# adaLN by column-tiled fp32 products spread over the layers, norms as diagonal products with a scale and a shift per feature

## The chip, the cores and the metric

One NeuronCore of a Trainium2 chip runs the whole program in one launch. The metric is device time in microseconds. Five engines work side by side, each through its own instructions in order: TensorE (PE, matrix products), VectorE (DVE), ScalarE (ACT), GpSimd (POOL, here mostly an issuer of DMAs) and SyncE (SP, which issues the loads of the weights). They hold each other up through semaphores: a count that one engine raises and another waits for.

## The reference, cut to what matters

Two transformer layers over 128 context tokens and 256 latent tokens, in fp32. Each layer derives six vectors of 1024 values, for the context and for the latent tokens, from a conditioning vector, and uses them around its two sublayers:

```python
def _adaln(cvec, w, b):
    m = (jax.nn.silu(cvec) @ w + b).reshape(-1, 1, 6 * D_MODEL)   # w: 1024 x 6144
    return jnp.split(m, 6, axis=-1)

mp, ms = _adaln(c_ctx, mod_w[i], mod_b[i]), _adaln(c, mod_w[i], mod_b[i])
hs = _rmsnorm(xs, norm1_g[i]) * (1 + ms[1]) + ms[0]      # the same for hp with mp
xs = xs + ms[2] * mixer(hs)
hs = _rmsnorm(xs, norm2_g[i]) * (1 + ms[4]) + ms[3]
xs = xs + ms[5] * ffn(hs)
```

Layer 0's mixer is windowed attention beside retention (one input projection of 2816 columns), its second half a dense SwiGLU. Layer 1's mixer is neighbourhood attention, its second half a top-2-of-8 expert SwiGLU, chosen by a router (`h @ w_router`, 1024 x 8, then top 2). One RMSNorm ends it.

## The kernel before, in words

The 384 tokens are three tiles of 128 rows (tile 0 context, 1 and 2 latent). A dense product runs on blocks of 128 x 1024 fp32 weights (512 KB). SP loads them into a ring of six raw buffers (`rawb`), ScalarE rounds each to `whi` (fp32r) and VectorE takes the rest, `wlo = raw - whi` (lines 464 and 469, three buffers each), and TensorE makes three products for one: hi x hi, lo x hi, hi x lo (lines 519 to 521). The experts do the same at lines 488 and 492 with eleven raw buffers, and besides run their overflow tokens by plain fp32 products on the raw block, 32 stationary columns wide, four side by side in the array (lines 1224 and 1242). Engines take blocks strictly in a numbered order.

The stages, in order: the twelve 512-column chunks of layer 0's adaLN (48 blocks, a loop at lines 1290 to 1299); two chunks of layer 1's (8 blocks); norm 0; the input projection, in whose block order the other 40 adaLN blocks of layer 1 stand two behind each weight block (`mod1`, lines 885 and 887); retention; attention of layer 0; output projection; norm 1; dense SwiGLU; norm 2; the QKV projection; attention of layer 1; output projection; norm 3; router; experts; last norm.

An adaLN block is converted like any other. Its products have the conditioning columns as stationary operand (hi and lo of both vectors) and stream 512 columns, two k-slices for each of hi and lo: four products. The rows go from PSUM to `mst`, and by a POOL DMA to `mods_scratch` in DRAM; from there POOL loads them back as rows of `mrow` (lines 705, 711, 717).

A norm (`norm_rows`, line 1746; `norm` on TensorE, line 870) works on token rows. TensorE spreads the scale and shift rows over 128 partitions by products with selector matrices (line 834), VectorE forms `h = x * rstd * scale` and `h + shift` for each tile (lines 1758 and 1764, 128 x 1024 each), TensorE turns `h` (line 866), ScalarE and VectorE make `hT_hi` and `hT_lo` out of PSUM, TensorE spreads the gate rows, and then the next product starts. `rstd` comes from ScalarE's squares of all three tiles (line 1380), one VectorE scaling (line 1748), one ScalarE root (line 1382), one reciprocal. The router takes 72 products that have the turned tokens as stationary operand and stream 8 columns.

Of the kernel before, what the change touches and what calls it, by code (L numbers as in the profile page):

```python
# [7 lines left out]
F32 = mybir.dt.float32  # L8
# [49 lines left out]
MOD_CH, MOD_STEP = 12, 3  # L58
B_MOD0 = 0
B_MOD1 = B_MOD0 + MOD_CH * SB  # L60
MOD_EARLY, MOD_PER = 2, 2
IN_BLOCKS = IN_EVEN * KD // BLK
B_OUT0 = B_MOD1 + MOD_CH * SB + IN_BLOCKS

N_MOD1, N_IN = [B_MOD1 + b for b in range(MOD_EARLY * SB)], []
while len(N_MOD1) + len(N_IN) < MOD_CH * SB + IN_BLOCKS:
    N_IN.append(B_MOD1 + len(N_MOD1) + len(N_IN))
    for _ in range(min(MOD_PER, MOD_CH * SB - len(N_MOD1))):
        N_MOD1.append(B_MOD1 + len(N_MOD1) + len(N_IN))
assert len(N_IN) == IN_BLOCKS and SB % MOD_PER == 0  # L70
# [5 lines left out]
assert IN_EVEN % 512 == 256 and EB % RAW == 0 and EB % HL == 0 and (MOD_STEP * SB) % RAW == 0  # L76
# [4 lines left out]
TURNED = {0: 0, 1: 6, 2: 9, 3: 15, 5: 21}  # L81
# [5 lines left out]
for _name, _n in (("ident", P), ("ones", P), ("before", P), ("slots", CAP), ("experts", E), ("orow", E), ("sel", 4 * P),  # L87
# [7 lines left out]
def constants():  # L95
# [15 lines left out]
    sel = np.zeros((4, 32, 4, P))  # L111
    for m, rows in enumerate(((0, 2, 4), (1, 3, 4), (0, 2, 4, 5), (1, 3, 4, 5))):
        for r in rows:
            sel[:, r, m] = 1
    put("sel", sel.reshape(P, 4 * P))
# [26 lines left out]
def build(nc, a, outs):  # L142
# [5 lines left out]
    mods = nc.dram_tensor("mods_scratch", [4, 2 * MOD_CH * 512], F32).ap()  # L148
# [4 lines left out]
    with ExitStack() as ctx:  # L153
# [27 lines left out]
        mrow = sb("mrow", [P, D])  # L181
        gate = sb("gate", [P, 2, D])
        gbc = sb("gbc", [P, D])
# [31 lines left out]
        moe_top = top[0] + 4 * BLK  # L215

        top[0] = act_at + 12 * 1024
        wr = sb("wr", [P, KD, E])
        wr_hi = sb("wr_hi", [P, KD, E], F32R)
        wr_lo = sb("wr_lo", [P, KD, E], F32R)  # L220
# [14 lines left out]
        ccol = sb("ccol", [P, 16])  # L235
        padrow = sb("padrow", [C_HEADS * DR, PADW])
        mst_at = act_at + 10 * 1024
        mst = sb("mst", [4, MOD_STEP, 512], at=mst_at)

        top[0] = act_at  # L240
        mr_hi = sb("mr_hi", [P, D], F32R)
        mr_lo = sb("mr_lo", [P, D], F32R)
        sel_r = sb("sel_r", [P, 4 * P], F32R)
# [8 lines left out]
        mst1 = sb("mst1", [4, 512])  # L252
# [56 lines left out]
        ident = cst("ident")  # L309


        cs_by_k = cs4[:, 0:4 * KD].rearrange("p (k c) -> p k c", c=4)


        w_loaded = [sem(f"w_loaded{i}") for i in range(RAW)]
# [1942 lines left out]
```

## Time and profile before

| | |
|---|---|
| median of 3 runs (lowest, highest) | 2025.83 us (2024.74, 2027.09) |
| the profiled execution: its own time, its span | 2025.68 us, 2023.6 us |
| PE busy, share of the span | 1800.2 us, 89% |
| DVE busy | 1231.9 us, 61% |
| ACT busy | 1074.8 us, 53% |
| moved by DMA, mean rate | 440.91 MB, 218 GB/s |
| mean granted TensorE clock | 0.935 |

A busy time is the time in which an engine had an instruction under way. The granted clock is a share of full speed (1.0 is 2.4 GHz, 0.5 is 1.2 GHz). All times of the trace are counted from the start of the span; the 2.1 us between span and time lie around it.

### The profile page before, as it was taken

Reading aid. Unit: us, or ns where it says so; the run is one execution under the profiler, and the core shown is the slowest. Engines: PE = TensorE matmul, PEld = TensorE weight load, DVE = VectorE, ACT = ScalarE, POOL = GpSimd, SP = SyncE. Lnnn points to the kernel's source line nnn. Section 1 sums busy time; section 2 is a strip of 40 time slices with the busy share of each in tenths; the row PEclk is TensorE's granted clock in tenths of the full one; section 3 lists DMA queues with packets and bytes.
Section 4 is the critical chain, followed back from the end, with each engine's and each line's share of the span. In section 5 each row is a group of like instructions: output and inputs, shape, how many; then the busy total and the mean of one; then the engine's idle time right before and its main releaser. Section 6 shows DMA issues by size and latency. Waiting matters only on the chain.

```text
span 2023.6 us, 26720 instructions
## 1 busy us (share of the span) xinstructions
PE 1800.2 (89%) x9765; PEld 1375.9 (68%) x9766; DVE 1231.9 (61%) x1430; ACT 1074.8 (53%) x1451; POOL 162.5 (8%) x262
## 2 busy tenths in 40 slices
PE   4868888889999989999799999999898989899890
PEld 2546676668888868767676656667676767677670
DVE  3764556653434252484446556578787878788783
ACT  3755543533332233463245545567676777677771
POOL 3010010030000040160010000000000000000002
PEclk9879997989999979999589999999999999999995
DMA  8946650158443445321168777799999989899883
GB/s 271 324 176 227 220 195 13 40 170 301 125 121 119 125 115 138 106 71 57 69 219 234 234 228 239 230 312 334 330 336 323 338 310 364 308 348 326 315 296 108
DMA packets 204805, 440.91 MB, mean 218 GB/s; under 512 B 16648, under 2 KB 36160, under 8 KB 204672
## 3 DMA queue, kind: packets, MB, share of 16 engines
q1 hardware_dynamic: 188928, 394.31, 58.4%
q0 software_dynamic: 15744, 44.73, 6.9%
q8 instruction: 95, 1.56, 0.3%
q14 instruction: 38, 0.31, 0.1%
HBM read 413.69 MB, written 25.30 MB: 217 GB/s over the span
## 4 chain that ended last, share of the span: by engine, by line
PE 74%; DVE 11%; ACT 7%; issue 4%; DMA 3%; POOL 0%; SPq 0%; ACTq 0%; DVEq 0%; POOLq 0%
PE ps L519 22%; PE ps L520 20%; PE ps L521 20%; PE ps L1224 3%; DMA rawb<-in_mod_w 2%; DVE wlo L469 2%; DVE wlo L492 2%; ACT whi L464 2%; ACT whi L488 2%; PE ps L968 1%; PE ps L1242 1%; PE ps L1187 1%; DVE h L1758 1%; PE ps L834 1%; DVE h L1764 1%
## 5 line engine op out<-in xcount | busy, mean ns | idle before, releaser
L469 DVE TENSOR_TENSOR wlo<-rawb,whi 128x1024 fp32r<-128x1024 f32 x224 | 269.6, 1223 | 346.6 <-ACT whi L464 345.5
L492 DVE TENSOR_TENSOR wlo<-rawb,whi 128x1024 fp32r<-128x1024 f32 x288 | 348.1, 1223 | 163.5 <-ACT whi L488 161.7
L464 ACT ACTIVATE whi<-rawb 128x1024 fp32r<-128x1024 f32 x224 | 232.1, 1056 | 350.2 <-PE ps L521 316.7
L488 ACT ACTIVATE whi<-rawb 128x1024 fp32r<-128x1024 f32 x288 | 303.9, 1061 | 154.3 <-PE ps L521 77.4
L492 DVE TENSOR_TENSOR wlo<-rawx,whi 128x1024 fp32r<-128x1024 f32 x240 | 289.5, 1223 | 89.9 <-ACT whi L488 88.7
L519 PE MATMUL ps<-whi,eT_hi 128*128 128x512 f32 (+1 forms) x768 | 311.2, 405 | 36.5 <-issue 27.3
L488 ACT ACTIVATE whi<-rawx 128x1024 fp32r<-128x1024 f32 x240 | 252.6, 1061 | 109.7 <-PE ps L521 52.3
L520 PE MATMUL ps<-wlo,eT_hi 128*128 128x512 f32 (+1 forms) x768 | 293.6, 382 | 0.0
L521 PE MATMUL ps<-whi,eT_lo 128*128 128x512 f32 (+1 forms) x768 | 292.4, 381 | 0.0
L519 PE MATMUL ps<-whi,hT_hi 128*128 128x512 f32 (+1 forms) x672 | 261.3, 389 | 17.1 <-DVE wlo L469 17.1
L521 PE MATMUL ps<-whi,hT_lo 128*128 128x512 f32 (+1 forms) x672 | 257.2, 383 | 0.0
L520 PE MATMUL ps<-wlo,hT_hi 128*128 128x512 f32 (+1 forms) x672 | 257.2, 383 | 0.0
L519 PEld LDWEIGHTS ps<-whi,eT_hi 128*128 128x128 f32 x768 | 148.9, 194 | 99.9 <-issue 43.1
L521 PEld LDWEIGHTS ps<-whi,eT_lo 128*128 128x128 f32 x768 | 148.9, 194 | 28.6
L519 PEld LDWEIGHTS ps<-whi,hT_hi 128*128 128x128 f32 x672 | 128.5, 191 | 51.2 <-DVE wlo L469 24.6
L520 PEld LDWEIGHTS ps<-wlo,eT_hi 128*128 128x128 f32 x768 | 149.4, 195 | 19.5
L519 PE MATMUL ps<-whi,eF_hi 128*128 128x512 f32 x352 | 145.6, 414 | 0.1
L521 PEld LDWEIGHTS ps<-whi,hT_lo 128*128 128x128 f32 x672 | 128.2, 191 | 24.8
L520 PEld LDWEIGHTS ps<-wlo,hT_hi 128*128 128x128 f32 x672 | 128.5, 191 | 23.2
L520 PE MATMUL ps<-wlo,eF_hi 128*128 128x512 f32 x352 | 139.2, 396 | 0.0
L521 PE MATMUL ps<-whi,eF_lo 128*128 128x512 f32 x352 | 139.1, 395 | 0.0
L519 PEld LDWEIGHTS ps<-whi,eF_hi 128*128 128x128 f32 x352 | 66.0, 187 | 35.6 <-issue 13.6
(304 smaller groups left out, 2167.4 us busy)
## 6 DMA issues: line engine op xcount, KB each, us to landing
rawb<-in_od_moe_w_gu SPq DMA_DIRECT2D x192, 512.0 KB, 5.5
rawx<-in_od_moe_w_gu SPq DMA_DIRECT2D x160, 512.0 KB, 5.8
rawb<-in_mod_w SPq DMA_DIRECT2D x96, 512.0 KB, 5.3
rawb<-in_od_moe_w_down SPq DMA_DIRECT2D x96, 512.0 KB, 5.1
rawx<-in_od_moe_w_down SPq DMA_DIRECT2D x80, 512.0 KB, 4.9
rawb<-in_ev_ffn_w_gu SPq DMA_DIRECT2D x44, 512.0 KB, 3.7
rawb<-in_od_w_qkv SPq DMA_DIRECT2D x24, 512.0 KB, 3.7
rawb<-in_ev_w_in SPq DMA_DIRECT2D x22, 512.0 KB, 3.7
```

Of the source, the lines that this page charges most:

```text
L464: nc.scalar.activation(whi[:, r, :], rawb[:, s, :], ACT.Copy).then_inc(hi_done, 1)
L469: nc.vector.tensor_tensor(wlo[:, r, :], rawb[:, s, :], whi[:, r, :].bitcast(F32), ALU.subtract).then_inc(lo_done, 1)
L488: nc.scalar.activation(whi[:, moe_slot(i), :], moe_raw(j), ACT.Copy).then_inc(hi_done, 1)
L492: nc.vector.tensor_tensor(wlo[:, moe_slot(i), :], moe_raw(i % EB), whi[:, moe_slot(i), :].bitcast(F32), ALU.subtract).then_inc(lo_done, 1)
L519: nc.tensor.matmul(out, l_hi, r_hi, start=start, stop=False)
L520: nc.tensor.matmul(out, l_hi, r_lo, start=False, stop=False)
L521: return nc.tensor.matmul(out, l_lo, r_hi, start=False, stop=stop)
L834: mm = nc.tensor.matmul(ps[:, b, :], sel_r[q:q + 6, m * P:(m + 1) * P], part[q:q + 6, 512 * half:512 * (half + 1)], start=(part is mr_hi), ...
L968: mm = nc.tensor.matmul(ps[:, 2 + u, c * P:(c + 1) * P], s_p[:, m % SLOTS[lay], u, c * P:(c + 1) * P], dg[:, m % 3, u, :], start=True, sto ...
L1187: mm = nc.tensor.transpose(ps[:, 6 + s % 2, c * P:(c + 1) * P], eg[:, c * P:(c + 1) * P], ident)
L1224: mm = nc.tensor.matmul(ps[q * OV:(q + 1) * OV, 2 + g, 0:P], oT[:, k, :], moe_raw(b)[:, c:c + P], start=(k == 0), stop=(k == KD - 1))
L1242: mm = nc.tensor.matmul(ps[q * OV:(q + 1) * OV, 2, 0:2 * P], oF[:, j, :], moe_raw(b)[:, q * 2 * P:(q + 1) * 2 * P], start=(j == 0), stop=( ...
```

## The change

- **adaLN rows.** All 96 blocks are now 128 rows by 1024 columns, read by TensorE raw, as fp32: no `whi`, no `wlo`. `mod_block` makes four products of 32 stationary and 256 streamed columns, side by side in the array. Sixteen blocks (shift and scale of norm 0) run before norm 0, 24 behind the weight blocks of the input projection (two behind each of the first four, then one), 24 within attention 0 (at steps 0 to 2, 4 to 6 and 9 to 11 of 15) and 32 within attention 1. SP loads everything by one list, `RING`, still into six buffers; a buffer is free after `wlo` for a weight block and after the product for an adaLN block.
- **Columns in place of rows.** For a shift or a scale, two turns (`mod_turn`) and a VectorE addition give a column per feature (`cols`, with bias, 1 + scale and the gain in it). For a gate the bias goes in by four more products, and `gate_rows` spreads it by eight fp32 products of 256 columns. These stand in the output projections, in the down-projection of the dense SwiGLU, and for the last gate among the router's work. The trip through DRAM is gone.
- **Norms.** VectorE makes `dgx`, a diagonal matrix of the tile's `rstd`; TensorE turns and scales at once, `x` (stationary) times `dgx`, 24 fp32 products for a norm. ScalarE and VectorE apply scale and shift per feature from PSUM into `vT`, then make `hT_hi` and `hT_lo` k-slice by k-slice; the next product starts with the first slice. Means and roots are taken tile by tile.
- **Router.** The weights (padded to 32 columns) are stationary, 8 fp32 products stream the 384 tokens; a small product with `fold` adds the four column groups. `rows_back` turns `vT` into rows of `h` for the experts.
- **POOL's DMAs.** The big constants, the small tables, the initial states and the zero rows of `rpb_scratch` are issued only after 12 adaLN blocks are used. ScalarE and VectorE wait for the end of that last one (`pad_out`) before norm 0 writes `vT`.

```diff
+RING = [("m", i) for i in range(2 * KD)]
+for _b in range(IN_BLOCKS):
+    RING += [("w", _b)] + [("m", i) for i in MODS_BEHIND[_b]]
+RING += [("w", B_OUT0 + i) for i in range(HL)] + [("m", i) for i in range(5 * KD, 8 * KD)]
...
+            pool.wait_ge(mod_used, 12)
             pool.dma_start(more[:, :], const[:, nkeep:NCONST]).then_inc(more_in, 16)
...
+            def mod_block(i):
+                qi, k = divmod(i, KD)
+                p = AT["m", i]
+                gate_row = qi in GATES and k == KD - 1
+                pe.wait_ge(w_loaded[p % RAW], 16 * (p // RAW + 1))
...
+                for g in range(4):
+                    mm = nc.tensor.matmul(ps[32 * g:32 * (g + 1), bank, 0:2 * P], cs[:, k, :], raw[:, 2 * P * g:2 * P * (g + 1)],
+                                          start=(k == 0), stop=(k == KD - 1 and not gate_row))
...
+            def norm(n):
                 for t in range(T):
+                    pe.wait_ge(ndg, T * n + t + 1)
+                    if t:
+                        pe.wait_ge(mc_v, 2 * (n + 1))
+                    for k in range(KD):
+                        own, both = normed_at(k)
+                        out = own if t == 0 else both[:, (t - 1) * P:t * P]
+                        mm = nc.tensor.matmul(out, x[:, t, k * P:(k + 1) * P], dgx[:, t, :], start=True, stop=True)
...
+                    for i in MODS_AT[lay].get(m, ()):
+                        mod_block(i)
...
             def norm_stats(n):
+                def root(t):
+                    act.wait_ge(nms, T * n + t + 1)
+                    nc.scalar.activation(st[:, 6 + t:7 + t], st[:, 3 + t:4 + t], ACT.Sqrt).then_inc(nsd, 1)
...
                     nc.scalar.activation(h[:, t, :], x[:, t, :], ACT.Square, accum_out=st[:, t:t + 1]).then_inc(nsq, 1)
-                act.wait_ge(nms, n + 1)
-                nc.scalar.activation(st[:, 6:9], st[:, 3:6], ACT.Sqrt).then_inc(nsd, 1)
+                    if t:
+                        root(t - 1)
+                root(T - 1)
...
+            def normed(n):
+                def high(k):
+                    act.wait_ge(nv1, KD * n + k + 1)
+                    act.wait_ge(nv0, KD * n + k + 1)
+                    nc.scalar.activation(hT_hi[:, k, :], vT[:, k, :], ACT.Copy).then_inc(nhi, 1)
+                act.wait_ge(mc_v, 2 * (n + 1))
+                for k in range(KD):
+                    act.wait_ge(nt2_ps, KD * n + (k | 1) + 1)
+                    nc.scalar.activation(vT[:, k, P:T * P], normed_at(k)[1], ACT.Identity, scale=scale_col(n, 1, k),
+                                         bias=shift_col(n, 1, k)).then_inc(nv1, 1)
```

GpSimd's queue at the start, before (`more`, `ck`, `lg`, `S`: constants and states that attention and retention need; `rpb_scratch` a scratch in DRAM):

```order
L661 DMA x<-in_x_prompt 128x1024
L662 DMA x<-in_x_sample 128x2x1024
L666 DMA mrow<-constants 1x8x128 [waits mr_z]
L666 DMA mrow<-constants 1x8x128 x2
L668 DMA more<-constants 128x1858
L669 DMA ck_117<-in_cache_a_k 128x128
```

and now (`bgate` and `brow` hold the biases and gains that the first addition needs):

```order
L677 DMA x<-in_x_prompt 128x1024
L678 DMA x<-in_x_sample 128x2x1024
L679 DMA bgate<-in_mod_b 48x256
L680 DMA brow<-in_mod_b 96x128
L682 DMA brow<-in_norm_g 8x128 x4
L683 MEMSET padrow 112x127
L684 MEMSET wr 128x256
L686 DMA more<-constants 128x1858 [waits mod_used]
L687 DMA ck_119<-in_cache_a_k 128x128
```

All that stood behind `more`, the write of `rpb_scratch` too, moved behind the twelfth adaLN block.

ScalarE at norm 1, before (`h` is only a place for the squares, `st` the sums):

```order
L1372 ACT_TABLE_LOAD
L1372 ACTIVATE st<-first 128x1
L1380 ACTIVATE h,st<-x 128x1024 [waits x_upd] x3
L1382 ACTIVATE st<-st 128x3 [waits nms]
L1393 ACTIVATE hT_hi<-ps 128x4x128 [waits tin_ps] x6
```

and now:

```order
L1401 ACT_TABLE_LOAD
L1401 ACTIVATE st<-first 128x1
L1409 ACTIVATE h,st<-x 128x1024 [waits x_upd] x2
L1399 ACTIVATE st<-st 128x1 [waits nms]
L1409 ACTIVATE h,st<-x 128x1024 [waits x_upd]
L1399 ACTIVATE st<-st 128x1 [waits nms] x2
L1424 ACTIVATE vT<-ps,cols 128x256 [waits nt2_ps,mc_v]
L1424 ACTIVATE vT<-ps,cols 128x256 [waits nt2_ps]
L1419 ACTIVATE hT_hi<-vT 128x384 [waits nv0,nv1]
```

The root of tile 0, which needs VectorE's mean, now stands ahead of the square of tile 2.

TensorE at the first steps of attention 0, before (`kT`, `qT`: scores; `dg`, `s_p`: weighting and turning of the softmax):

```order
L959 MATMUL ps<-kT,qT 128x128 x2
L959 MATMUL ps<-kT,qT 128x384 x2
L940 MATMUL ps<-keep,proj_115 128x128 x3
L959 MATMUL ps<-kT,qT 128x384 x2
L968 MATMUL ps<-dg,s_p_143 128x128 x2
L959 MATMUL ps<-kT,qT 128x128 x2
```

and now:

```order
L961 MATMUL ps<-kT,qT 128x128 x2
L823 MATMUL ps<-rawb,cs 32x256 x12
L961 MATMUL ps<-kT,qT 128x384 x2
L933 MATMUL ps<-keep,proj_117 128x128 x3
L823 MATMUL ps<-rawb,cs 32x256 x12
L961 MATMUL ps<-kT,qT 128x384 x2
L970 MATMUL ps<-dg,s_p_144 128x128 x2
L823 MATMUL ps<-rawb,cs 32x256 x8
```

Three, three and two adaLN blocks (line 823, four products each) came between the scores of one step and those of the next.

## Rows read from the trace of the kernel before

**Rows 1.** Busy time by stage: stretch, length, then each engine's busy us, clock, DMA.

```profile
core 0: us, PE busy (x) PEld busy (x) DVE busy (x) ACT busy (x) POOL busy (x), PEclk, DMA share, GB/s
...
11.00:107.00 96.00, 64.70 (x193) 40.45 (x194) 57.80 (x50) 56.35 (x62) 8.61 (x16) 0.93 0.92 309
...
118.00:141.30 23.30, 13.42 (x48) 9.96 (x48) 15.66 (x18) 11.22 (x19) 4.07 (x8) 0.52 0.36 132
141.30:296.00 154.70, 137.60 (x592) 107.48 (x592) 81.40 (x85) 85.19 (x118) 5.19 (x10) 0.97 0.62 205
...
342.00:393.00 51.00, 41.28 (x304) 31.27 (x305) 37.42 (x103) 29.52 (x77) 0.15 (x1) 0.91 0.04 11
...
420.00:439.70 19.70, 12.77 (x50) 8.12 (x49) 17.58 (x22) 9.34 (x16) 4.18 (x8) 0.66 0.27 86
...
725.00:745.00 20.00, 14.68 (x42) 9.03 (x42) 17.45 (x23) 7.16 (x13) 9.94 (x18) 0.54 0.42 114
...
845.00:935.00 90.00, 80.36 (x630) 59.26 (x629) 66.04 (x133) 56.26 (x149) 38.26 (x47) 0.96 0.19 49
...
963.00:985.00 22.00, 14.07 (x48) 9.89 (x48) 13.88 (x19) 10.27 (x16) 1.51 (x2) 0.56 0.35 126
985.00:998.40 13.40, 13.39 (x63) 13.30 (x63) 1.15 (x8) 0.00 (x0) 0.00 (x0) 0.50 0.01 1
```

**Rows 2.** DMA issues by tensor, whole run: count, size, median us to landing.

```profile
rawb<-in_mod_w SPq DMA_DIRECT2D x96, 512.0 KB, 5.3
...
rpb_scratch<-padrow POOLq DMA_DIRECT2D x1, 55.6 KB, 18.2
```

**Rows 3.** GpSimd's timeline from the start: start us, length, line, what.

```profile
6.12 0.57 POOL L668 DMA_DIRECT2D more<-constants  x1
...
14.26 0.65 POOL L684 DMA_DIRECT2D rpb_scratch<-padrow  x1
```

**Rows 4.** TensorE's timeline inside one down-projection block of an expert.

```profile
1161.70 0.40 PE L521 MATMUL ps<-whi,eF_lo 128*128 128x512 f32 x1
1162.03 0.64 PE L1242 MATMUL ps<-rawb,oF 128*32 128x256 f32 x8
1162.60 0.50 PE L519 MATMUL ps<-whi,eF_hi 128*128 128x512 f32 x1
```

**Rows 5.** TensorE's timeline in the input projection, one adaLN block.

```profile
147.88 0.39 PE L885 MATMUL ps<-whi,cs 128*128 128x512 f32 x1
...
148.80 0.40 PE L885 MATMUL ps<-whi,cs 128*128 128x512 f32 x1
```

**Rows 6.** TensorE's waits between 141 and 296 us: us, times, longest.

```profile
PE ps L519 <- DVE wlo L469: 17.1, 20, 2.5
```

**Rows 7.** TensorE's timeline in the first attention.

```profile
355.85 1.60 PE L968 MATMUL ps<-dg,s_p 128*128 128x128 f32 x12 [1.40 <-DVE dg L1909]
357.38 0.44 PE L992 MATMUL ps<-s_pT,proj 128*64 128x128 f32 x4
```

**Rows 8.** TensorE's timeline at the second norm (layer 0).

```profile
419.73 0.39 PE L521 MATMUL ps<-whi,hT_lo 128*128 128x512 f32 x1
...
439.66 0.80 PE L519 MATMUL ps<-whi,hT_hi 128*128 128x512 f32 x1
```

**Rows 9.** VectorE's timeline at the same norm.

```profile
424.14 1.22 DVE L469 TENSOR_TENSOR wlo<-rawb,whi 128x1024 fp32r<-128x1024 f32 x1
425.94 0.17 DVE L1748 TENSOR_SCALAR st<-st 128x3 f32<-128x3 f32 x1 [0.58 <-ACT h L1380]
```

**Rows 10.** TensorE's timeline at the start of the first attention.

```profile
341.91 0.80 PE L959 MATMUL ps<-kT,qT 64*128 64x128 f32 x4 [2.06 <-DVE s_p L1885]
```

**Rows 11.** TensorE's timeline after routing.

```profile
1001.29 2.73 PE L1333 MATMUL ps<-msk,keep 128*128 128x8 f32 x12 [2.90 <-DVE msk L2116]
...
1007.46 8.38 PE L1144 MATMUL ps<-oh,h 128*128 128x128 f32 x48 [2.17 <-DVE oh L2032]
```

**Rows 12.** VectorE's timeline at the last norm.

```profile
2005.37 1.22 DVE L2229 TENSOR_TENSOR x<-x,acc 128x1024 f32<-128x1024 f32 x1
```

More of the change, by code:

```diff
@@ L57 @@
 PITCH = CAP + XT * P
[L58 to L61, printed above, removed]
+B_IN = 0
 IN_BLOCKS = IN_EVEN * KD // BLK
[L63 to L70, printed above, removed]
+B_OUT0 = B_IN + IN_BLOCKS
 B_FFN = B_OUT0 + 2 * SB
@@ L109, in constants @@
     put("orow", np.tile(np.arange(E) * PITCH, (P, 1)))
[L111 to L115, printed above, removed]
+    put("fold", np.tile(np.eye(32, E), (4, 1)))
     nf = DH // 4
@@ L892, in dense, with ready @@
+            def normed(n):
+                def ready(k):
+                    if k == 0:
+                        pe.wait_ge(nv0, KD * (n + 1))
+                    pe.wait_ge(nlo, KD * n + k + 1)
+                return ready
+            def dense(ch, base, before_last=None, ready=None, gi=None):
+                bank = BK if base is not None else range(6)
                 for c, (bs, o, n) in enumerate(ch):
@@ L1109, in feed @@
                     rows = BLK // n
-                    if g and not s:
-                        pe.wait_ge(gate_ev, 2)
                     for i in range(nb):
@@ new lines, in _ @@
+            pe.wait_ge(mc_v, ahead_of(NQ))
+            dense(OUT_CH[1], None, ready=lambda k: pe.wait_ge(at_lo, 4 + k + 1), gi=2)
+            norm(3)
+            pe.wait_ge(wr_in, 16)
+            for rnd in range(2):
+                for g in range(4):
+                    k = 4 * rnd + g
+                    pe.wait_ge(nv0, KD * 3 + k + 1)
+                    pe.wait_ge(nv1, KD * 3 + k + 1)
+                    mm = nc.tensor.matmul(ps[32 * g:32 * (g + 1), 4, 0:T * P], wr[:, k, :], vT[:, k, :], start=(rnd == 0),
+                                          stop=(rnd == 1))
@@ L1779, in dense @@
             def dense(ch, extra=None, n=None, hold=False):
                 for c, (bs, o, w) in enumerate(ch):
-                    last = min((N_MOD1[mod_behind(bs[-1])[-1]] if mod_behind(bs[-1]) else bs[-1]) + 1 + HL, B_MOE)
+                    last = min(bs[-1] + 1 + HL, B_MOE)
+                    for qi, end in ENDS_BEHIND.items():
+                        if qi not in GATES and end + 2 in bs:
+                            ahead.to(end + 2 + HL)
+                            mod_cols(qi)
                     if n is not None:
```

804 lines of the change are left out of this document (404 added, 400 removed).

## The prediction

> **What bounds the kernel now.** I read the busy time by stage first [rows 1]. Up to 141.3 us no token product runs: 48 + 8 adaLN blocks pass, then norm 0. From 11 to 107 us the DMA share is 0.92 at 309 GB/s with TensorE busy 64.70 of 96 us: loading bounds that stretch, conversion nearly does. The input projection takes 154.70 us, TensorE busy 137.60, and its waits for `wlo` sum to 17.1 [rows 6]. The dense stages after it run TensorE nearly full; the three norms between them are holes of 19.70, 20.00 and 22.00 us at clock 0.54 to 0.66 [rows 1]. In the attentions TensorE is busy 41.28 of 51 and 80.36 of 90 us, so little is free there. Experts and their weights don't change. So the sum has five places: the start, the input projection, the attentions, the norms with their gates, the router.
>
> **Start: the first token product moves from 141.3 to about 47 us (-94).** What must be loaded before norm 0 is 16 blocks of 0.524 MB, the tokens (1.57), constants (0.29) and biases (0.1): 10.4 MB. At 309 GB/s [rows 1] that is 34 us from about 1.5 us on: 36 us. One block's four products cost 0.57 us, from 1162.03 to 1162.60, where the experts run this very shape (32 stationary, 256 streamed columns, four groups; 8 records) [rows 4]; even at half clock, 1.1, they keep up with a block each 1.6 us. Copy, turns and addition of the last columns: 1.5 us, so 38.6. Then come 24 fp32 products of 128 columns before the first token product, in TensorE's order. The routing's gather has 24 like them (48 records) in 8.38 us after a pause [rows 11]; warm they are 1.53 / 6 = 0.255 us each [rows 7], together 6.1. I take 8.4: 47 us.
>
> Beside it runs a chain that is new on this path: `pad_out`. POOL issues from `more` to the write of `rpb_scratch` in 14.26 - 6.12 = 8.1 us, and that write took 18.2 us to land [rows 2, 3] with more queued around it. Now it starts at the twelfth used block, near 30 us: 38 + 2 to 18, so 40 to 56. I take 44, hidden behind the 24 products; at 56 the start is 58, the slow end (-83). The fast end, loads a tenth above 309 GB/s (what is left above a share of 0.92) and warm products, is 41 (-100).
>
> The Trainium skill, "DMA: Bandwidth & Descriptors", section "Anatomy of one DMA — SWDGE (gpsimd) path", fits a transfer as 2.0 us plus bytes at 436 GB/s. By it 10.4 MB would take 26 us instead of 34 and the whole would come out 8 us lower. The trace has 5.3 us for a block of 512 KB while several are under way [rows 2], where that rule gives 3.2 for one alone; I stay with the stretch's own rate.
>
> **Input projection: 154.7 to about 121 us (-34).** Out go 40 interleaved adaLN blocks, each four products at 0.23 us (148.80 - 147.88 = 0.92) [rows 5]: 37.1. Out go the 17.1 us of waits [rows 6], since ScalarE and VectorE convert 22 blocks instead of 62. In come 24 blocks at 0.57 = 13.7, and a price for leaving the full array: in rows 4 the fp32 group starts 0.33 after the product before it, which alone takes 0.23, and the first product behind it takes 0.50 instead of 0.39. That is 0.2 us a visit, 22 visits: 4. I add 3 us of waits at the beginning, where ScalarE finishes eight slices of norm 0 before converting the second block. 154.7 - 37.1 - 17.1 + 13.7 + 4 + 3 = 121. Bounds: 114 without price and waits, 130 with half the old waits left.
>
> The Trainium skill, "TensorEngine Tiling (Array Packing)", section "Tiling Modes", says that changing the tiling mode drains TensorE. The row has it at 0.2 us a visit. Without the rule the 78 or so visits of the whole kernel would be free and the time 10 to 15 us lower.
>
> **Attentions: +24.** 24 blocks x 0.57 = 13.7 and 32 x 0.57 = 18.2 us of new TensorE work where nothing stood. TensorE's idle there is 9.7 and 9.6 us [rows 1], in pieces that wait for the softmax, such as 2.06 us in the first steps [rows 10], and the new blocks stand between a step's scores and the next's, so only part disappears. In attention 0 there is one ring stall too: block 45's buffer is that of the third output weight, which is converted only at the end of step 1, and a load takes some 4 to 5 us [rows 2]. I take +11 and +13. Bounds: 0, if all falls into idle time or a busier array is granted a higher clock (0.91 and 0.96 now), and 56 x 1.1 = +62 at half clock, nothing hidden.
>
> **Gates: +11.** Three of four gates become eight fp32 products of 256 columns inside stages that are full. A record of 128 columns is 0.1275 [rows 7]; 256 columns lie between that and twice it; I take 0.235, two records a product: 8 x 0.47 = 3.8 us, three times. Bounds 6 to 13; any wait for ScalarE's copies would add to it.
>
> **Norms 1 and 2: -5 and -4.** Before, VectorE finishes its last conversion (424.14 + 1.23) and sends its mean at 425.94; the FFN starts at 439.66 [rows 8, 9]. Now tile 0's mean can leave at 425.4, but the root of tile 0 stands ahead of tile 2's square on ScalarE. `dgx` of tile 0 is ready about 426.6 and that of tile 2 about 429, hidden because TensorE needs 8.4 us for 24 products: 435, then slices flow. 439.7 - 435 = 4.9 less; norm 2, alike in shape, 4.4. What took the 20 us before, VectorE's six passes over 128 x 1024, is gone; what ends last now is TensorE's 24 fp32 products. Warm they would save 2 more in each, fully cold (0.43 each) 2 less.
>
> **Norm 3 and router: -9.** The 72 router products fill the 13.40 us from 985.0 at clock 0.5 [rows 1]. Now: diagonal products end near 976, eight products of 384 columns end near 978, rows back (three times 2 us), eight gate products at half clock (7) and position products (1003.87 + 1.43 - 1001.29 = 4.0, [rows 11]) with ScalarE's copies between: the positions end near 996.5 against 1005.3. Bounds -4 to -14.
>
> **Last norm: +1.** VectorE adds the last tile until 2006.6 [rows 12] and only then sends tile 0's mean, and tile 2's square now waits behind tile 0's root.
>
> **Sum.** -94.3 - 33.7 + 24 + 11.4 - 4.9 - 4.4 - 9 + 1 = -109.9. From the profiled execution's 2025.7 that is 1915.8; the median, 2025.83, is the same. Forecast: 1916 us.
>
> **Rivals.**
> - *The attentions swallow their blocks.* Idle time, and a clock nearer 1.0, cover nearly all of 32 us, and the start is at its fast end. For it: 19.3 us of idle in the two stages. Against: dependences tie it to the softmax. 1916 - 24 = 1892, or 1886 with a faster start.
> - *The start runs late or the attentions lengthen.* `pad_out` at 56 us gives 1927; every block delaying a softmax chain (+32 instead of +24, the ring stalls repeated) 1935 to 1940.
> - *The column groups don't run side by side for TensorE in these stages.* Four times 0.57 a block over some 80 blocks beside other work: +137, so 2053, slower. Rows 4 speak against it: eight records take 0.57 us.
> - *The ring starves in the attentions (slower).* Six buffers are used in order; if each of the 56 blocks there waited a whole landing of 5.3 us [rows 2], they would cost 297 us and not 24: 2189. Without the attentions the change gains 134 us, so it decides from 2.4 us a block on. Against it: blocks are one buffer each, six are in flight, and the DMA share in both stages is low (0.04 in the first, [rows 1]).
>
> **Chances.** Forecast (1902 to 1928) 0.55; attentions swallowed or quicker start, below that, 0.23; late start or longer attentions 0.19; the two slower ones together 0.02; that nothing moves 0.01. The range, 1888 to 1938, leaves out about two in ten and takes in the start's ends and most of the attentions' bounds. A change under 0.2% (4 us) can't be told from none here; faster 0.97, same 0.01, slower 0.02.
>
> **What would show it.** In the changed kernel's profile: the first token product at 47 us, with either TensorE's diagonal products or `pad_out` as what ended last; 121 us to the end of the input projection with hardly a wait for `wlo`; the attentions at 62 and 103 us; no VectorE pass over 128 x 1024 in the norms, and holes of 15 us instead of 20. I am wrong if token products start after 60, if adaLN blocks in the attentions show waits for DMA after the first group, or if a stage I called unchanged (retention, experts) moves by over 3 us.

## The result, and the profile after

The changed kernel takes 1915.2 us (median of 4 runs, 1914.78 to 1920.43), beside 2026.46 us for the kernel before: ratio 0.9458, 95% interval 0.944 to 0.9476. The forecast was 1916. The profiled execution took 1915.45 us, its span is 1913.7 us (2023.6 before), so the sum can be laid against two traces, stage by stage.

I cut both traces at the same events: the first token product, the first scores of an attention, the first product of a projection. The table has the start of each (us) and how much longer or shorter the stage that ends there became; the last column is the prediction's term.

| event that ends the stage | before | after | stage changed by | predicted |
|---|---|---|---|---|
| first token product | 141.33 | 58.44 | -82.9 | -94.3 |
| retention begins (input projection over) | 297.33 | 171.03 | -43.4 | -33.7 |
| first scores, attention 0 | 331.62 | 206.72 | +1.4 | 0 |
| output projection 0 | 387.17 | 273.08 | +10.8 | +11 |
| FFN (gates, norm 1) | 439.66 | 326.64 | +1.1 | -1.1 |
| second layer's projection (gates, norm 2) | 745.15 | 630.72 | -1.4 | -0.6 |
| first scores, attention 1 | 846.60 | 734.03 | +1.9 | 0 |
| output projection 1 | 928.30 | 831.75 | +16.0 | +13 |
| gather (gates, norm 3, router) | 1007.46 | 898.51 | -12.4 | -5.2 |
| first expert product | 1026.76 | 917.37 | -0.4 | 0 |
| end of the span | 2023.6 | 1913.7 | -0.5 | +1 |

That the sum came within 1 us is luck: the start is 11.4 us later than forecast, the input projection 9.7 us shorter, the router stretch 7.2 us shorter, and the remaining stages together 5.6 us longer. The mechanisms held in the main; the sizes cancel.

Busy time by stage in the changed kernel answers to [rows 1]; columns as there.

```profile
0.00:37.00 37.00, 14.86 (x132) 4.63 (x133) 2.62 (x20) 7.00 (x15) 11.52 (x26) 0.90 0.83 308
37.00:58.40 21.40, 6.76 (x51) 6.56 (x50) 4.78 (x13) 4.65 (x10) 5.58 (x9) 0.66 0.69 194
58.40:171.00 112.60, 111.56 (x636) 81.15 (x636) 41.86 (x57) 48.19 (x84) 0.00 (x0) 0.98 0.66 220
...
206.70:273.10 66.40, 53.90 (x502) 34.09 (x502) 43.75 (x120) 31.09 (x89) 0.00 (x0) 0.87 0.55 199
...
611.00:630.70 19.70, 7.84 (x48) 7.67 (x49) 14.30 (x31) 8.36 (x17) 7.36 (x13) 0.65 0.36 120
...
734.00:829.50 95.50, 87.25 (x843) 57.51 (x843) 62.50 (x131) 54.16 (x148) 34.78 (x40) 0.98 0.68 214
...
880.00:898.50 18.50, 14.92 (x105) 11.79 (x104) 7.79 (x42) 13.83 (x21) 0.00 (x0) 0.94 0.08 29
```

Read three things. In the input projection TensorE is busy 111.56 of 112.60 us, where it was 137.60 of 154.70: nothing waits there now. Between 37 and 58.4 us TensorE is busy 6.76 of 21.40 us at a clock of 0.66, though the products of the last of the first 16 blocks start at 36.0: that is the hole that I had put at 11 us. And the stretch with the router, 985.0 to 998.4 at clock 0.50 before, runs at 0.94.

What fills the hole is shown by the chain of waits from 30 to 62 us, followed back from the first token products (start, length, what):

```profile
32.31 0.57 POOL more L686
...
38.10 2.36 POOL S L698 x4
40.45 14.71 DMA rpb_scratch<-padrow
...
55.19 2.64 DVE vT L1814 x8
57.83 0.48 DVE hT_lo L1819
```

GpSimd waits for the twelfth used block until 32.3, issues 14 loads, and only then the write of zeros to `rpb_scratch`. That write of 55.6 KB takes 14.71 us; VectorE stands at its wait ahead of the norm's slices until 55.19. It is the chain that the prediction put at 40 to 56 us and took at 44.

Some of TensorE's waits in the whole changed kernel, as groups (us, times, longest):

```profile
PE ps L862 <- DVE dgx L1796: 22.4, 3, 11.2
PE ps L823 <- DMA rawb<-in_mod_w: 17.8, 9, 7.9
PE ps L534 <- DVE hT_lo L1819: 16.0, 3, 14.2
...
PE ps L1298 <- DMA brow<-in_norm_g: 8.1, 1, 8.1
...
PE ps L933 <- ACT kT L1500: 3.5, 2, 2.8
PE ps L534 <- DVE wlo L484: 3.2, 2, 1.6
```

The first is the three later norms, before their diagonal products. The third is the hole. Of the second, 7.9 and 4.8 us are two stalls in the attentions, one in each, both early ("ring stalls" below: the ring's next buffer isn't loaded yet):

```profile
220.47 1.08 PE L823 MATMUL ps<-rawb,cs 128*32 128x256 f32 x8 [7.91 <-DMA rawb<-in_mod_w]
...
745.98 1.03 PE L823 MATMUL ps<-rawb,cs 128*32 128x256 f32 x8 [4.82 <-DMA rawb<-in_mod_w]
```

Of the small additions two are in these waits as well: 2.8 us in the second layer's projection (L933), where the turns of the queries now wait for the copy of the keys (`kT`), and twice 1.6 us for `wlo` in the output projections, because VectorE waits for ScalarE's gate copy in front of that conversion.

### The profile page after: what moved, and what is told of

Read it like the earlier page. It is cut to its first block, busy times and chain, and to the rows that moved or that the text cites. A ratio compares the mean times of both kernels' runs of the same rounds, so it can differ in the third digit from the quotient of the medians.

```text
span 1913.7 us, 27142 instructions
## 1 busy us (share of the span) xinstructions
PE 1717.9 (90%) x10236; PEld 1308.8 (68%) x10237; DVE 1100.2 (57%) x1372; ACT 982.0 (51%) x1391; POOL 141.8 (7%) x222
## 4 chain that ended last, share of the span: by engine, by line
PE 81%; DVE 7%; ACT 5%; issue 3%; DMA 3%; POOL 1%; DVEq 0%; ACTq 0%; POOLq 0%
PE ps L534 23%; PE ps L535 20%; PE ps L536 20%; PE ps L1234 3%; DVE wlo L507 2%; PE ps L823 2%; ACT whi L503 2%; PE ps L970 2%; PE ps L1252 1%; PE ps L1197 1%; PE ps L961 1%; PE ps L862 1%; PE ps L994 1%; DMA rpb_scratch<-padrow 1%; DMA rawb<-in_mod_w 1%
## 5 line engine op out<-in xcount | busy, mean ns | idle before, releaser
L507 DVE TENSOR_TENSOR wlo<-rawb,whi 128x1024 fp32r<-128x1024 f32 x288 | 348.1, 1223 | 164.0 <-ACT whi L503 162.4
L503 ACT ACTIVATE whi<-rawb 128x1024 fp32r<-128x1024 f32 x288 | 303.9, 1061 | 154.0 <-PE ps L536 77.7
L484 DVE TENSOR_TENSOR wlo<-rawb,whi 128x1024 fp32r<-128x1024 f32 x128 | 157.6, 1234 | 292.3 <-ACT whi L479 291.8
L479 ACT ACTIVATE whi<-rawb 128x1024 fp32r<-128x1024 f32 x128 | 135.4, 1060 | 321.2 <-PE ps L536 267.1
```

The lines of the kernel that those rows point to most:

```text
L479: nc.scalar.activation(whi[:, r, :], rawb[:, s, :], ACT.Copy).then_inc(hi_done, 1)
L484: nc.vector.tensor_tensor(wlo[:, r, :], rawb[:, s, :], whi[:, r, :].bitcast(F32), ALU.subtract).then_inc(lo_done, 1)
L503: nc.scalar.activation(whi[:, moe_slot(i), :], moe_raw(j), ACT.Copy).then_inc(hi_done, 1)
L507: nc.vector.tensor_tensor(wlo[:, moe_slot(i), :], moe_raw(i % EB), whi[:, moe_slot(i), :].bitcast(F32), ALU.subtract).then_inc(lo_done, 1)
```

## The experiments

Small differences need a yardstick better than the span. In the profiled executions of the variants whose routing is unchanged, the stretch from the first expert product to the end took 995.7 to 1000.8 us, though none touches it. So I give the whole time with its ratio to the kernel before, and beside it when the first expert product started (917.4 us in the changed kernel). That event isn't exact either: in the two executions of one kernel, `best` and `best_again` below, it comes at 896.1 and 891.4. A difference of 3 us in it shows nothing by itself; the stage with the edit has to be looked at.

### Three waits, taken away singly

**pad_early** issues the padded write ahead of GpSimd's wait:

```diff
+            pool.wait_ge(pad_z, 1)
+            pool.dma_start(padded, padrow[:, :]).then_inc(pad_out, 16)
             pool.wait_ge(mod_used, 12)
...
-            pool.wait_ge(pad_z, 1)
-            pool.dma_start(padded, padrow[:, :]).then_inc(pad_out, 16)
             pool.wait_ge(pad_out, 16)
```

> POOL writes the zero rows of rpb_scratch ahead of its wait for twelve adaLN blocks; nothing else moves. Theory A (the first token product, at 58.4 us, waits for that write alone, queued behind 14 DMAs): TensorE's diagonal products end at 44.3 in the changed kernel, so the input projection starts at 45.5 to 46.5 and the time falls by 12 to 13 us, to about 1902.5. Rival B (the late DMAs as such, the big constants above all, hold the start or the first chunk's tables): the start moves by less than half, or the 13 us come back as waits in the input projection, time above 1909.

Measured: 1906.93 us, ratio 0.9417 (0.9397 to 0.9437); first expert product at 909.7. The first token product moved from 58.44 to 44.79, by 13.7 us, a little more than expected, and 2 us before the 47 that I had predicted with the write hidden. The whole gained only 8.3 us where I had expected 12 to 13, since 4.8 us came back: the input projection took 117.4 us in place of 112.6. The chain of waits (columns as above):

```profile
25.27 8.14 DMA rawb<-in_mod_w
...
34.16 19.04 DMA rawb<-in_ev_w_in
...
53.22 1.06 ACT whi L479
...
54.31 1.24 DVE wlo L484
...
55.59 0.50 PE ps L534
```

The second weight block is issued at 34.16 and lands 19.04 us later; TensorE waits 3.9 us for it, and 15 token products instead of 10 then start 0.43 us apart, at half clock, and not 0.23, which is the other us. In the changed kernel the late start had covered that. Why it takes 19 us is the question of the last group below.

**pool_free** leaves the wait for the twelfth block out, so that all of GpSimd's loads go out from 8 us on:

```diff
-            pool.wait_ge(mod_used, 12)
```

> POOL issues all its first DMAs at once, without the wait for twelve adaLN blocks. Theory A (holding them back costs more here than it gives): the write of rpb_scratch lands near 30 us as before the change, 1.4 MB of other loads delay the sixteen blocks by 4 to 5 us at 309 GB/s, so the first token product comes at 49 to 51 us and the time is 1906 to 1908. Rival B (small loads slow the block loads out of proportion, as the first 30 us of the kernel before suggest): start at 58 us or later, time 1915 or above.

Measured: 1912.88 us (1905.33 to 1914.4), ratio 0.943 (0.9405 to 0.9455), missing the expected 1906 to 1908. The write landed by 28.9, but the 16 blocks came 6 us later (the products of the last start at 41.8 in place of 36.0), and the first token product started at 49.66. The first expert product is at 909.3, as in pad_early; the two differ behind it (1000.8 against 995.7 us), in the stretch that neither touches. On the part that the edits concern they are equal; loads kept out of the start save 5 us there and cost 5 in the input projection.

**conv_early** lets ScalarE and VectorE convert the first pieces of the output weights ahead of each attention's loop, so that the buffers that the blocks need come free:

```diff
+                ahead.to((B_OUT0, B_OUT1)[lay] + HL)
                 for m in range(N + lag + 2):
...
-                    if m == 1:
-                        ahead.to((B_OUT0, B_OUT1)[lay] + HL)
```

> ScalarE and VectorE convert the third output weight before an attention's first step, not at step 1. Theory A (the 7.9 and 4.8 us that TensorE waits for an adaLN block come from that buffer being freed late, the loads behind it in SP's order included): both waits go, attention 0 from 66.4 to about 59, attention 1 from 97.7 to about 93, and the time falls by 9 to 12 us, to about 1905. Rival B (these are the price of six buffers and a landing of 5 to 6 us, whenever the buffer comes free): a wait of at least 4 us stays in each, time above 1911.

Measured: 1907.42 us, ratio 0.9418 (0.9402 to 0.9434); first expert product at 908.1. TensorE's waits for blocks fall from 17.8 to 6.8 us over the kernel:

```profile
PE ps L823 <- DMA rawb<-in_mod_w: 6.8, 8, 2.0
```

Attention 0 took 59.5 us in place of 66.4, attention 1 94.8 in place of 97.7; the whole gained 7.8 us where I had expected 9 to 12. So 7 of the +10.8 us and 3 of the +16.0 were ring stalls and not products; the stall in attention 0 cost 7.9 us and not the 4 to 5 that I had counted. What is left for the blocks themselves is 59.52 - 55.55 = 4.0 us in attention 0 and 94.78 - 81.70 = 13.1 in attention 1 (the second number of each is the kernel before).

**gates_early** has ScalarE copy the gate rows half a chunk earlier:

```diff
-                        if gi is not None and (c, i) in ((1, 0), (1, 2)):
-                            gate_rows(gi, i)
+                        if gi is not None and (c, i) in ((0, 3), (1, 1)):
+                            gate_rows(gi, 2 * c)
```

> ScalarE copies the spread gate rows one conversion earlier, in both output projections. Theory A (VectorE's additions wait for that copy, its conversions queue behind them, and TensorE waits 1.6 us in each output projection): both waits go, the time falls by 3 us, to 1912. Rival B (the conversions are late because ScalarE's own are, so the copy ahead of them costs what it saves): 1914 to 1916.

Measured: 1912.48 us, ratio 0.9435 (0.942 to 0.9451); first expert product at 914.1. The two waits of 1.6 us are gone, and the two stretches that begin with the output projections are shorter by 1.8 and 1.0 us. The gain of 2.7 us in the whole can't be told from none: the interval overlaps that of the changed kernel, and attention 0, which the edit does not touch, came out 1.6 us shorter as well.

### What a visit of TensorE to an adaLN block costs

Three kernels change the four products of a block. The adaLN rows differ from the reference's in all three, and so does the routing: in `double` and `one_of_four` more passes over the experts run. Their whole times (2924.58 and 2436.47 us) therefore say nothing; the events up to the first expert product do. In `one_group` the number of passes stayed, but the gather of the overflow (9 us) fell away ahead of the first expert product, and the experts took 1003.1 us instead of 996.3.

`double` issues each of the four twice, `one_group` sends all four to column group 0 for six of eight blocks, `one_of_four` issues one of four for six of eight blocks in the attentions:

```diff
 double
-                for g in range(4):
+                for j in range(8):
+                    g = j % 4
...
-                                          start=(k == 0), stop=(k == KD - 1 and not gate_row))
+                                          start=(k == 0 and j < 4), stop=(k == KD - 1 and j > 3 and not gate_row))
 one_group
+                    q = g if k in (0, KD - 1) else 0
-                    mm = nc.tensor.matmul(ps[32 * g:32 * (g + 1), bank, 0:2 * P], cs[:, k, :], ...
+                    mm = nc.tensor.matmul(ps[32 * q:32 * (q + 1), bank, 0:2 * P], cs[:, k, :], ...
 one_of_four
-                for g in range(4):
+                for g in range(4) if i < 5 * KD or k in (0, KD - 1) else (3,):
```

> Every adaLN block's four products are issued twice (the sums of the adaLN rows double; nothing else changes), so that a visit holds eight products in place of four. Theory A, column time on TensorE: a visit costs about 0.77 us now (0.2 to enter and leave the tiling, 0.57 for the four products); four more cost 0.48 to 0.57. The 16 blocks ahead of the token work are bound by their DMAs and give at most 0.5; the 24 blocks of the input projection give 11.5 to 13.7; the 56 blocks of the two attentions give 27 to 32, less the 7.9 + 4.8 us of waits for blocks that are there already. Together 1943 to 1955 us. Rival B, the attentions are bound by ScalarE's and VectorE's chain or by the blocks' DMAs and the products lie in their shadow: only the input projection pays, 1927 to 1929 us. Rival C, a product of 32 columns needs only a quarter of the time, 0.12: the visit grows by 0.12 and the sum is under 1925 us.

> For six of the eight blocks of each adaLN quarter all four products go to column group 0 in place of groups 0 to 3 (the adaLN rows come out wrong; as many products of the same shape). Theory A, the four groups run side by side: one product of 256 columns in fp32 has 4 x 256 rows to stream, 0.43 us at 2.4 GHz, so four in one group take 1.7 us where four groups take 0.48 to 0.57. 60 of the 72 changed blocks are behind the start: 18 x 1.2 = 22 us in the input projection, 42 x 1.2 = 50 us in the attentions, less up to 12.7 us of waits there: 1975 to 1987 us, and the 12 in the start could add 0 to 10. Rival B, the four are served one after another anyway, each in a quarter of the time because 32 of 128 columns are used: no change, 1913 to 1918 us.

> In the two attentions, for six of the eight blocks of each quarter, only the fourth of the four products is issued (the adaLN rows come out wrong: three of four products of 42 blocks are left out); block loads, waits and the change of tiling stay. Theory A, side by side: a lone product still takes about 0.43 of the 0.48 to 0.57 us, so 42 visits save 0.05 to 0.14 each, 2 to 6 us: 1909 to 1913 us, and what the attentions have grown by is the visits' fixed part and the waits for blocks. Rival B, one after another: a visit shrinks by three quarters of 0.57, 42 x 0.43 = 18 us less, 1897 to 1901 us.

Times in us; the rows below the first are differences to it.

| | start | input projection, retention | attention 0 | attention 1 | first expert product |
|---|---|---|---|---|---|
| after | 58.4 | 148.3 | 66.4 | 97.7 | 917.4 |
| double | +2.2 | +11.2 | +7.8 | +12.4 | +34.6 |
| one_group | +5.5 | +23.2 | +16.0 | +25.2 | +62.3 |
| one_of_four | +0.1 | +0.1 | -1.5 | +0.1 | -2.4 |

TensorE's time in these products over the whole kernel (line and shape, count of records, two for a product, busy us, mean ns, idle before): the changed kernel,

```profile
L823 PE MATMUL ps<-rawb,cs 128*32 128x256 f32 x768 | 61.3, 435 | 17.8 <-DMA rawb<-in_mod_w 17.8
```

`double`,

```profile
L824 PE MATMUL ps<-rawb,cs 128*32 128x256 f32 x1536 | 99.8, 399 | 13.5 <-DMA rawb<-in_mod_w 13.4
```

`one_group`,

```profile
L824 PE MATMUL ps<-rawb,cs 128*32 128x256 f32 x768 | 149.5, 395 | 6.2 <-DMA rawb<-in_mod_w 6.2
```

and `one_of_four`:

```profile
L823 PE MATMUL ps<-rawb,cs 128*32 128x256 f32 x516 | 60.0, 441 | 17.5 <-DMA rawb<-in_mod_w 17.5
```

A block's four products take 61.3 / 96 = 0.64 us; four more add (99.8 - 61.3) / 96 = 0.40; the same number in one group takes (149.5 - 24 x 0.64) / 72 = 1.86. So four groups run side by side, and one of the four products alone costs nearly as much as all of them: leaving out 126 of 168 in the attentions took TensorE's time in them from 61.3 to 60.0 us. The 1.4 us by which the attentions shortened (2.4 up to the first expert product) are no more than stages vary by without an edit. In the trace two blocks together fill the step to the next scores in 1.00 us; with one product in place of four in one of them (10 records for 16), 0.98:

```profile
240.06 1.07 PE L823 MATMUL ps<-rawb,cs 128*32 128x256 f32 x16
241.06 0.92 PE L961 MATMUL ps<-kT,qT 64*128 64x384 f32 x4
```

```profile
240.41 1.05 PE L823 MATMUL ps<-rawb,cs 128*32 128x256 f32 x10
241.39 0.92 PE L961 MATMUL ps<-kT,qT 64*128 64x384 f32 x4
```

`double` fell in with theory A stage by stage: 24 blocks x 0.40 is 10 in the input projection (11.2 measured), 32 blocks 13 in attention 1 (12.4), and attention 0 takes 7.8 of 10, so some of it fell into idle time. Its rival, that products added there lie in the shadow of the softmax, is refuted for these added ones. The first four of each block in attention 0 do lie there for the most part: without the ring stall they lengthen it by 4.0 us (conv_early), though they take 13.3 from start to start. `one_group` has 18 x 1.22 = 22 us for the input projection (23.2), 29 for attention 1 (25.2), 22 for attention 0 (16.0). Its whole time, 1984.42 us (ratio 0.9786, 0.9763 to 0.9809), is 69 us above the changed kernel's, within the expected 1975 to 1987.

### Together, and what slows the second weight block

**best** has the three edits pad_early, conv_early and gates_early.

> The three edits tried singly, together: the padded write issued ahead of the wait for twelve blocks, the first pieces of the next projection's weights converted ahead of the attention loops, and the gate rows copied earlier. Singly they gave -8.4, -7.8 and -2.8 us against the changed kernel. Theory A, they lie in different stages and add: 1915.2 - 19.0 = 1896 us, 1894 to 1899. Rival B, earlier conversion and earlier start share one cause (the DMA ring): what pad_early gained is lost again at the blocks of the first attention, where conversions of weights now take slots earlier: 1901 to 1905 us.

Measured: 1894.28 us, ratio 0.9343 (0.9327 to 0.9358), first expert product at 896.1; once more, in the run beside the next two (**best_again**), 1892.62 us, ratio 0.9346 (0.9333 to 0.9359). They add, as theory A had it: 20.9 us where the single ones sum to 18.8.

> The three edits together once more, beside the two above on the same chip: 1894 us, 1892 to 1896, first token product at 44.6 and first scores at 199.8 us.

What is left is the wait of 4.7 us (6.5 in best_again) before the second weight block's products: input projection and retention take 155.2 us in place of 148.3, 4.7 by the wait and the rest by products at half clock (21 start 0.43 us apart, where the changed kernel has 10). From 40 to 50 us the DMA engines of `best` are busy at 0.75 and move only 148 GB/s:

```profile
40.00:50.00 10.00, 8.16 (x42) 6.91 (x41) 7.89 (x17) 7.20 (x17) 1.73 (x3) 0.83 0.75 148
```

I put it down to the loads of GpSimd. **best_late** issues all of them behind the second converted weight block, those of the decay logits first:

```diff
-            pool.wait_ge(mod_used, 12)
+            pool.wait_ge(lo_done, RAW + 2)
```

> On top of the three edits together: all of GpSimd's later loads (the second part of the constants, keys and values, decay logits, states, relative biases, router weights) wait until the second weight block of the input projection is converted, in place of the twelfth used adaLN block. Theory A, these loads, 0.93 MB and 14 small ones, share the DMA engines with the weight blocks issued at 31 and 34 us, which took up to 19 us to land: the wait of 4.7 us before the second block's products goes to under 1, the input projection takes 149 to 151 us to the first scores in place of 155.2, and the time is 1888 to 1890 against 1894.3. Rival B, the blocks are late because SyncE issues them late or ScalarE converts them late: no change, 1893 to 1896. Rival C, the loads only collide later, with blocks issued from 51 us on: the wait moves by some ten us and the time stays.

**best_small_late** leaves the large one, the 0.93 MB of constants, at the twelfth used block and moves the small ones.

> As best_late, but the second part of the constants, one load of 0.93 MB, stays at the twelfth used block; only the 14 small loads wait. If the many small loads delay the weight blocks (40 to 50 us moved 50 to 200 GB/s at a high busy share), this is as fast as best_late, 1888 to 1890. If it is the large one, the time is that of the three edits, 1894, and the wait stays 4 to 5 us. If both by their bytes (0.93 and 0.5 MB), two thirds of the gain are missing: 1892.

Measured: best_late 1897.55 us, ratio 0.9371 (0.9358 to 0.9383); best_small_late 1895.78 us, ratio 0.936 (0.9347 to 0.9373). Both are slower than best_again, measured beside them, by 4.9 and 3.2 us. Theory A was right about the cause and wrong about the gain. Without the loads the same bytes pass from 40 to 50 us at a share of 0.37 in place of 0.75 (best_late),

```profile
40.00:50.00 10.00, 9.05 (x57) 8.22 (x56) 5.59 (x14) 5.96 (x14) 0.00 (x0) 0.91 0.37 143
```

and the second weight block lands in time. The DMA issues between 34 and 36 us give its landing (count, size, us to landing). In `best`:

```profile
rawb<-in_ev_w_in SPq DMA_DIRECT2D x1, 512.0 KB, 19.9
```

In best_late it takes 7.1 us, and in best_small_late, where the large load is still beside it, 9.7:

```profile
rawb<-in_ev_w_in SPq DMA_DIRECT2D x1, 512.0 KB, 9.7
```

But now the block issued at 61 to 63 us, beside the small loads, is the slow one. The chain of waits in best_late:

```profile
62.89 13.50 DMA rawb<-in_ev_w_in
...
76.41 1.06 ACT whi L479
...
77.50 1.24 DVE wlo L484
...
78.78 0.80 PE ps L534
```

and in best_small_late:

```profile
60.92 13.84 DMA rawb<-in_ev_w_in
```

In best_late TensorE does no token product between 68.4 and 78.78 us. That is rival C: the slow stretch moves with the loads. The large load isn't the culprit, since the block beside it landed in 9.7 us.

**best_split** asks which small loads: the six of the decay logits stay at the twelfth used block, the nine others wait until 86 us. (The expectations say 14 and 10 small loads; there are 15, and nine of them wait here.)

```diff
             pool.dma_start(more[:, :], const[:, nkeep:NCONST]).then_inc(more_in, 16)
-            pool.dma_start(ck0[:, :], ...    (with cv0 and sinks)
             for d, src in enumerate((lg_f, lg_b)):
...
+            pool.wait_ge(lo_done, RAW + 8)
+            pool.dma_start(ck0[:, :], ...    (with cv0 and sinks)
             for d, src in enumerate((st_f, st_b)):
```

> On top of the three edits together: constants and decay logits stay at the twelfth used adaLN block; keys, values, sinks, states, relative biases and router weights (10 small loads, 0.46 MB) wait until the eighth weight block of the input projection is converted, near 86 us, when the blocks' loads no longer fill the engines. Theory A, these ten are what slows a block beside them (20 us to land in place of 6 to 9), and near 90 us six blocks in the ring cover it: the second weight block lands by 45, the wait of 4.7 to 6.5 us before it goes to under 2 (ScalarE's slices of norm 0 end then), no new wait near 62 us, first scores at 194 to 196 us, 1889 us, 1886 to 1891. Rival B, the six tiny strided loads of the decay logits do it: the wait stays near 5, 1893 to 1895 us. Rival C, a ring of six blocks doesn't cover a slow stretch at 90 us either: the wait appears there, 1895 to 1898 us.

Measured: 1893.62 us, ratio 0.9337 (0.9325 to 0.935), first expert product at 895.1. Rival B: the block is as late as ever.

```profile
34.33 18.74 DMA rawb<-in_ev_w_in
...
53.09 1.06 ACT whi L479
```

Beside it ran only the large load, which best_small_late had cleared, and the six loads of the logits, 4 KB twice and 1 KB four times. By best_small_late and best_split together these six slow a block of 0.5 MB from 9.7 to 18.7 us. Four of them fetch every second of a direction's 8 logits for each of 64 partitions, single numbers of 4 bytes; two spread the 8 logits in one piece. No run separates these, but the traces' records of the packets do. In `best` the four leave 64 packets of 64 bytes, 16 numbers each, from 40.5 to 51.6 us; they take 0.82 us each, 52.2 us of the 16 engines' time together. The 48 packets of 256 bytes, the two broadcasts and the sinks, take 2.8 us together. From 40 to 50 us the packets of 64 bytes alone are 49.3 us of 160, a share of 0.31, and that is most of the step from 0.37 to 0.75. In every trace they take 40 to 54 us together, wherever they are issued. A fetch of the logits as one contiguous row, spread over the partitions on chip, or ahead of the token loads, was not tried; it could recover up to the 5 us (an estimate from that wait).

`best` beats both kernels given: 1894.28 against 1915.2 and 2026 us. `best_split` can't be told from it.

## Why the prediction was right, and where its steps were not

- **Start, -94.3 against -82.9.** "I take 44, hidden behind the 24 products" failed: the write landed at 55.2, at the end of the range that I had given. With the write out of the way the start is 44.8. Beyond that the times held: the products of the last block start at 36.0 (predicted 36), and the 24 products run from 38.0 to some 44 us (6.3; I had taken 8.4). The mean rate, 308 GB/s, agrees with the 309 that I had taken, but by luck:

```profile
5.00:15.00 10.00, 0.26 (x1) 0.18 (x1) 0.00 (x0) 1.67 (x3) 2.92 (x7) 1.00 1.02 403
16.00:19.00 3.00, 1.68 (x13) 0.78 (x17) 0.96 (x5) 2.76 (x6) 0.00 (x0) 1.00 0.00 0
20.00:37.00 17.00, 11.92 (x114) 3.14 (x106) 0.73 (x4) 0.40 (x2) 4.68 (x9) 0.77 0.98 365
```

  The loads run at 403 and 365 GB/s, and between 16 and 19 us nothing moves. TensorE uses its first block at 17.7, behind its wait of 8.1 us for the rows of biases and gains (`brow`, L1298, above), and until a block is used no buffer of the six comes free. Blocks used ahead of those rows might bring the start some 3 us forward; that is an estimate from the pause, and not tried.

  By the Trainium skill's fit ("DMA: Bandwidth & Descriptors", "Anatomy of one DMA — SWDGE (gpsimd) path"), which is for GpSimd's transfers while SyncE issues the blocks, the estimate was that they are in by 28 us; the trace has 36. An estimate by the same fit gives 2.1 us for the small write, which is GpSimd's; it took 14.71 behind the other loads.
- **Input projection, -33.7 against -43.4.** The terms for what comes in were too large. 24 blocks cost 14.0 us from start to start of the rows, where I had 13.7 + 4 for leaving the full array + 3 of waits. The waits did not come because the late start covered them: with the write early they do (3.9 us, pad_early), so this error and that of the start are in part one. The token products took 98.6 us, and 98.4 before. The 0.2 us a visit is in the rows, 0.32 instead of 0.23 ahead of a visit and 0.33 instead of 0.23 behind it:

```profile
111.03 0.39 PE L536 MATMUL ps<-whi,hT_lo 128*128 128x512 f32 x1
111.35 0.64 PE L823 MATMUL ps<-rawb,cs 128*32 128x256 f32 x8
111.92 0.50 PE L534 MATMUL ps<-whi,hT_hi 128*128 128x512 f32 x1
112.25 0.39 PE L535 MATMUL ps<-wlo,hT_hi 128*128 128x512 f32 x1
```

  But the kernel before paid the second half too, behind adaLN products on the full array (start to start 0.33):

```profile
150.51 0.50 PE L519 MATMUL ps<-whi,hT_hi 128*128 128x512 f32 x1 [0.62 <-DVE wlo L469]
150.84 0.39 PE L520 MATMUL ps<-wlo,hT_hi 128*128 128x512 f32 x1
```

  New is only the 0.09 us ahead of a visit, 1.8 us for 20 of them, and 8 fewer token products at half clock give 1.6 back (10 start 0.43 us apart, 18 before). What goes out is 57.6 us where [rows 5, 6] gave 54.2. The Trainium skill has it that changing the tiling mode drains TensorE ("TensorEngine Tiling (Array Packing)", "Tiling Modes"); the trace agrees as far as those 0.09 us a visit.

- **Attentions, +24 against +26.8.** Right in size, and in attention 0 by luck: I had 6 to 7 us of products and a ring stall of 4 to 5 there, and the runs show 4.0 and 7 (conv_early). In attention 1 there was a stall of which I had nothing, 3 of the +16. The products take about 15 and 17 us from start to start, and fill idle time of the softmax: TensorE's waits for it fell from 14.2 to 5.1 us in attention 0 and from 9.5 to 3.4 in attention 1. So the rival that the blocks are swallowed is nearly right for attention 0, ring stall apart, and wrong for attention 1 (+13.1).
- **Gates, +11.4.** A product of 256 columns takes two records of 0.236 us, 3.8 us for the eight of a stage:

```profile
L848 PE MATMUL ps<-mqg,keep 128*128 128x256 f32 x64 | 15.1, 379 | 0.0
```

  15.1 / 4 = 3.8. The wait that I named without a size came twice, 1.6 us (gates_early).
- **Norms 1 and 2, -4.9 and -4.4.** With the gates the two stretches should have changed by -1.1 and -0.6 and did by +1.1 (the wait of 1.6 is in it) and -1.4. The hole at norm 1 is 15 us long, as I had said. That at norm 2 is 20 (610.7 to 630.7), not "alike in shape": TensorE waits 11.2 us for the first diagonal there, and 6.2 at norm 1.
- **Norm 3 and router, -5.2 with its gates against -12.4.** The mechanism held, the clock did not: I had taken half clock for products that ran at 0.94. Without the gate of the output projection, which lies in this stretch too (3.8 us), it gained 16.2 us where I had 9, outside the bounds of 4 to 14 that I had given. The eight 384-column products and what follows answer to [rows 11]:

```profile
875.15 7.55 PE L862 MATMUL ps<-dgx,x 128*128 128x128 f32 x48 [5.05 <-DVE dgx L1796]
882.63 3.53 PE L1332 MATMUL ps<-vT,wr 128*32 128x384 f32 x16
886.10 1.09 PE L1339 MATMUL ps<-keep,vT 128*128 128x128 f32 x8
...
888.52 1.89 PE L848 MATMUL ps<-mqg,keep 128*128 128x256 f32 x8
```

  Rows back take 1.09 us each where I had 2, the gates 2 x 1.89 where I had 7.
- **What I called unchanged.** Retention +1.4, experts and last norm -0.5; the second layer's projection +1.9, of which the prediction had nothing: a wait of 2.8 us for `kT` is new there, which no run takes away.
- **The rivals.** "The groups don't run side by side" was priced at +137 us over some 80 blocks; in one_group, where 72 blocks go so, a block costs 1.22 us more (98 us for 80 blocks) and not 1.71, since I had multiplied the whole visit by four; behind the start its 60 blocks added 64 us. The starving ring was real in two places, not in 56.

## What to carry to other kernels

When a change takes a long stage off the front, list every small chain that had been hidden in it (here a write of 55.6 KB issued behind 14 loads, 11 us) and issue those first. Work spread over a latency-bound stage needs its buffers free there before it begins; 7 of 11 us in the first attention were that and not the work. A few loads of single numbers doubled the landing time of a large one beside them: moving them only moved the slow stretch. And a forecast that comes out right in the sum has to be opened stage by stage: here errors of 11, 10 and 7 us cancelled.

## What the runs showed of the hardware that I had not expected

- Six loads of 12 KB together slow a block of 512 KB from 9.7 to 18.7 us to land; the DMA share is 0.75 at 148 GB/s beside the small loads and 0.37 at 143 GB/s without them. Their 64 packets of 64 bytes, 16 numbers each, take 0.82 us each in `best`.
- Of four fp32 products on the four column groups, three are nearly free: 126 left out took 1.3 us off TensorE's time in them, 0.01 each. Four in one group take 1.86 us, in four groups 0.64.
- The same stretch of experts, 996 us long, varies by 5 us between executions of kernels that are alike in it, and so does what stands ahead of it between two executions of one kernel (891.4 and 896.1 us).
